# Layer 1 of a two-layer diffusion backbone: projection, latent heads and both attentions as one stage of head pairs

## The chip, the cores and the metric

The kernel runs on one core of a Trainium2 chip. The metric is the device time of one execution in microseconds (us), less being better. The engines are PE (TensorE: matrix products into PSUM; PEld is its load of the stationary operand), DVE (VectorE), ACT (ScalarE), POOL (GpSimd) and SP (SyncE, which here only issues transfers). ACTq, SPq and POOLq are the instruction queues of those engines where they issue a transfer. PSUM has eight banks of 128 partitions by 512 float32 numbers. Everything is float32.

## What is computed

384 tokens (128 context tokens, 256 latent ones on a grid of 4 rows by 64 columns) go through two layers. Each layer is a mixer and then a mixture of 32 experts. The change lies in the mixer of layer 1, which has two attentions of eight heads side by side:

```python
def odd_mixer(h, j, P, cache):
    zq, zkv, zpe, nq, nk, nv = split_cols(h @ P['odd_w_in'][j], ODD_SPLITS)   # 256, 128, 32, 512, 512, 512
    ckv = rmsnorm(zkv, P['mla_kv_a_g'][j])
    q = mla_queries(zq, ...)      # rmsnorm, @ w_q_up (256 x 768), rmsnorm per head of 96, rotation
    k, v = mla_keys(ckv, zpe, ...)  # @ w_kv_up (128 x 1024), rmsnorm per head of 96, rotation
    nq = rmsnorm(nq.reshape(B, T, NAT_HEADS, HEAD_DIM), P['nat_q_g'][j])
    nk = rmsnorm(nk.reshape(B, T, NAT_HEADS, HEAD_DIM), P['nat_k_g'][j])
    y_mla = dense_attention(q, concat([k_c, k]), concat([v_c, v]))
    y_nat = neighbourhood_attention(nq, nk, nv, nk_c, nv_c, P['nat_rpb'][j])
    return concat([y_mla, y_nat]) @ P['odd_w_out'][j]
```

Context tokens attend to the 128 context keys alone, latent tokens to 128 cached keys and the 256 latent ones. In the neighbourhood attention every latent score gets a bias `rpb[head, row distance, column distance]`, and keys outside a window of 16 columns are masked out. The tokens are three tiles of 128 rows (t = 0 context, t = 1, 2 latent), so a unit of attention is one head of one tile: a product of scores (128 queries by 128 or 384 keys), a softmax, and a product with the values.

## The kernel before

All stages of a layer are blocks with one instruction stream per engine; `end_stage` ends one, and the engines meet there. Weights come in units of up to 2 MB through a ring of six slots (`T.ring`), which SP fills in the order of `weight_units`; a slot is filled again when PE has finished the unit in it, so behind the four units of `odd_w_in` and the two of `odd_w_out` come the first units of layer 1's experts. Layer 1's mixer has these stages:

- `stage_projection` (L640 to L750): the square sums of x, three normalized tiles, their transposes (`Turns`, L363, copied out with the modulation at L318 and L322), and then 12 jobs of eight products: unit n of `odd_w_in` by tile t (L739). `OddNorms` normalizes the latents and the neighbourhood queries and keys after the unit that holds them; the power of -0.5 is POOL's (L613).
- `stage_mla_heads` (L1823 to L1966): three groups of transposes of the latents, 6 jobs for the queries (L1957) and 8 for keys and values (L1960), then on DVE the sums, the scaling, the gain and the rotation of q and of k (L1929, L1935, L1938, L993, L997), with POOL for the powers (L1907) and for the cosine products (L1898). Then the transposes of q and k, 16 groups, whose copies ACT and DVE take in turn (L387).
- `stage_mla_attention`: class `Attention` (L827 to L972) for 24 units, one head of one tile each, in software pipeline: scores of unit i (L860), transposes of the probabilities of unit i-1 (L868), values of unit i-2 (L879, the transposed probabilities being the stationary operand). DVE takes the maximum (L936) and the shift (L947), ACT the exponential with its sum (L913), ACT and DVE copy the transposes in turn (L896). After eight heads DVE divides (L972) and writes rows of `mix`. The scores alternate between two banks, so the scores of unit i wait for the exponential of unit i-2.
- `stage_neighbourhood` (L1998 to L2110): transposes of nq and nk, among them of the cached keys, which ACT loads when the stage begins (L2036); 32 small transfers that spread the bias table over the partitions (L2052, 20 on SP, 12 on POOL); then the same `Attention`. In its first eight units `between` puts a product with a flip matrix (L2105) and a DVE pass (L2081) for the bias of two heads of one tile; the first of them waits for all 32 transfers. The scores get the bias in DVE's masked pass (L941).
- `stage_output` (L755): six groups of transposes of `mix`, then the output product (L816) and the gated residual.

Layer 0's window attention already runs on another class, `PairAttention` (L1005 to L1136), which takes two heads at a time with two score banks for both, divides in a diagonal matrix that stands in for the identity in the transpose (L1046, L1114), and writes the result transposed, so that no transposes follow. Products of the projection are put into its gaps.

The first waits of the two kinds of attention are these lines:

```python
if i >= 2:                                             # Attention, two score banks, one per unit
    pe.wait_ge(self.s_prob.sem, self.s_prob.at(i - 1))
...
if i >= 1:                                             # PairAttention, two score banks, both per step
    if self.steps[i - 1][3] is None:
        pe.wait_ge(self.s_prob.sem, self.s_prob.at(i))
```

## Time and profile before

| What | us |
|---|---|
| Median of 2 timed runs | 1868.99 (1868.97 to 1869.01) |
| The profiled execution, its own time | 1868.74 |
| Span of its trace | 1866.9 |
| PE busy in the span | 1416.1 (76%) |
| DVE, ACT, POOL busy | 534.8, 283.4, 246.1 |
| Mean granted PE clock, share of full speed | 0.891 |

Times in the trace are counted from the start of the span; 1.8 us of the execution lie outside it. PE's two clock levels are 1.2 and 2.4 GHz; the granted clock of a stretch is given as a share of the higher one, so 0.50 is the lower. Busy time of PE is that of instructions in flight, and a float32 product is issued as two instructions. The share of an engine is a mean over stages that have different limits, so what a change in one stage is worth has to be read inside that stage.

### The profile page before, as it was taken

The page shows a single profiled execution, that of the slowest core. Times are in us where ns is not written, and L with a number is a line of the kernel's source. Part 1 is how long each engine was busy: PE and PEld are TensorE (multiplying, and loading weights), DVE is VectorE, ACT ScalarE, POOL GpSimd, SP SyncE. Part 2 cuts the span into 40 slices and gives each one's busy share as a digit, 9 for nine tenths or more (in the row PEclk, how much of TensorE's full clock was granted, in tenths as well). Part 3 has the DMA queues.
Part 4 walks back from the last instruction along what each step waited for, and adds up shares of the span by engine and source line. Part 5 has one row for each costly group of instructions (what it writes and reads, how often), then busy time and mean ns, then how long its engine had stood idle before and what let it go on. Part 6 is the DMA issues. An engine that isn't in the chain of part 4 may idle for free. (4 is left out here: it accounts for less than half of the span.)

```text
span 1866.9 us, 19168 instructions
## 1 busy us (share of the span) xinstructions
PE 1416.1 (76%) x7912; PEld 778.7 (42%) x7912; DVE 534.8 (29%) x1013; ACT 283.4 (15%) x664; POOL 246.1 (13%) x237
## 2 busy tenths in 40 slices
PE   4999896749877777778079575998398777777772
PEld 3544443335444444444034253564154444444441
DVE  1142233452222222222222452322522222222222
ACT  2123335101000000000021232211010000000000
POOL 0100000222111111101102302000311111111101
PEclk9999998759999999999579876568599999999996
DMA  9637669329999999999722104002289999999994
GB/s 345 238 114 250 199 215 398 105 83 424 425 426 424 426 425 424 425 422 394 282 75 98 45 2 64 0 35 93 81 343 424 424 425 426 424 424 426 424 410 161
DMA packets 116073, 524.88 MB, mean 281 GB/s; under 512 B 39468, under 2 KB 44524, under 8 KB 91408
## 3 DMA queue, kind: packets, MB, share of 16 engines
q1 hardware_dynamic: 87216, 498.03, 66.1%
q0 software_dynamic: 10752, 13.49, 2.2%
q10 hardware_dynamic: 18016, 12.11, 2.1%
q8 instruction: 64, 1.05, 0.2%
q14 instruction: 25, 0.20, 0.0%
HBM read 521.37 MB, written 23.15 MB: 292 GB/s over the span
## 5 line engine op out<-in xcount | busy, mean ns | idle before, releaser
L2453 PE MATMUL ps<-ring,e_xT 128*64 128x256 f32 x4096 | 493.1, 392 | 120.2 <-DMA ring<-in_moe_w_gate 66.0
L2453 PEld LDWEIGHTS ps<-ring,e_xT 128*64 128x64 f32 x4096 | 303.2, 135 | 332.1 <-issue 118.4
L2467 PE MATMUL ps<-ring,e_hidT 128*64 128x512 f32 x1024 | 235.5, 601 | 53.8 <-DMA ring<-in_moe_w_down 53.8
L2511 POOL DMA_INDIRECT expert_rows<-e_y,table x64 | 64.7, 1011 | 794.9 <-DVE e_y L2628 785.1
L2467 PEld LDWEIGHTS ps<-ring,e_hidT 128*64 128x64 f32 x1024 | 79.4, 137 | 165.6 <-issue 116.5
L2628 DVE COPY e_y<-ps 128x512 f32<-128x512 f32 x64 | 44.3, 692 | 313.8 <-PE ps L2467 313.8
L1334 PE MATMUL ps<-ring,hT 128*128 128x512 f32 (+1 forms) x288 | 119.7, 571 | 5.0 <-ACT hT L318 5.0
L2636 DVE RECIPROCAL e_sig<-e_sig 128x256 f32<-128x256 f32 x64 | 112.2, 1753 | 2.2
L2634 DVE TENSOR_SCALAR e_sig<-e_sig 128x256 f32<-128x256 f32 x64 | 18.9, 295 | 312.9 <-ACT e_sig L2595 312.9
L2595 ACT ACTIVATE e_sig<-ps 128x256 f32<-128x256 f32 x64 | 24.5, 383 | 550.2 <-PE ps L2453 550.2
L739 PE MATMUL ps<-ring,hT 128*128 128x512 f32 (+1 forms) x192 | 81.4, 588 | 1.5 <-ACT hT L318 1.5
L1334 PEld LDWEIGHTS ps<-ring,hT 128*128 128x128 f32 x288 | 54.6, 194 | 61.4 <-issue 54.2
L2505 POOL DMA_INDIRECT x_in<-h_rows,table x64 | 65.8, 1029 | 83.1 <-issue 38.6
L2598 ACT COPY e_hidT<-ps 128x256 f32<-128x256 f32 x64 | 23.8, 372 | 300.3 <-PE ps L2459 300.3
L816 PE MATMUL ps<-ring,mixT 128*128 128x512 f32 x144 | 65.0, 615 | 1.6 <-issue 1.6
L363 PE MATMUL ps<-const,h 128*128 128x128 f32 x48 | 10.5, 401 | 73.3 <-DVE h L718 48.9
L2641 DVE TENSOR_TENSOR e_hid<-e_sig,ps 128x256 f32<-128x256 f32 x64 | 27.0, 421 | 111.0 <-PE ps L2453 111.0
L739 PEld LDWEIGHTS ps<-ring,hT 128*128 128x128 f32 x192 | 37.5, 196 | 45.2 <-issue 43.3
L395 PE MATMUL ps<-ring,cond 128*32 128x512 f32 x384 | 50.6, 648 | 6.9 <-ACT z L424 3.9
L2441 PE MATMUL ps<-const,x_in 128*128 128x128 f32 x256 | 42.8, 291 | 10.2 <-DMA x_in<-h_rows,table 10.2
L816 PEld LDWEIGHTS ps<-ring,mixT 128*128 128x128 f32 x144 | 28.4, 198 | 37.2 <-issue 36.1
L363 PE MATMUL ps<-const,mix 128*128 128x128 f32 (+1 forms) x61 | 14.1, 403 | 39.1 <-DVE mix L997 19.7
(329 smaller groups left out, 1390.4 us busy)
## 6 DMA issues: line engine op xcount, KB each, us to landing
ring<-in_moe_w_gate SPq DMA_DIRECT2D x64, 2048.0 KB, 26.8
ring<-in_moe_w_up SPq DMA_DIRECT2D x64, 2048.0 KB, 26.9
ring<-in_moe_w_down SPq DMA_DIRECT2D x64, 2048.0 KB, 27.0
ring<-in_ada_w SPq DMA_DIRECT2D x24, 2048.0 KB, 11.7
ring<-in_even_w_in SPq DMA_DIRECT2D x5, 2048.0 KB, 18.5
ring<-in_odd_w_in SPq DMA_DIRECT2D x3, 2048.0 KB, 26.6
rows<-expert_rows SPq DMA_DIRECT2D x12, 512.0 KB, 9.1
ring<-in_even_w_out SPq DMA_DIRECT2D x2, 2048.0 KB, 12.0
```

The costliest lines, as they stand in the source:

```text
L395: ins = T.nc.tensor.matmul(T.ps[32 * j:32 * (j + 1), bank, :], T.cond[:, c, :], T.unit(u)[:, c, :], start=(c < 4), stop=(c >= 4))
L739: ins = nc.tensor.matmul(T.ps[:, 4 + e % 4, 0:cols], hT[:, c, t * P:(t + 1) * P], T.unit(first + n)[:, c, :], start=(c == 0), stop=(c == K ...
L816: ins = nc.tensor.matmul(T.ps[:, 4 + e % 4, :], mixT[:, 4 * halves[k] + c, t * P:(t + 1) * P], T.unit(u)[:, c, n * 512:(n + 1) * 512], sta ...
L1334: ins = nc.tensor.matmul(T.ps[:, bank[e], 0:cols], hT[:, c, t * P:(t + 1) * P], T.unit(u)[:, c, :], start=(c == 0), stop=(c == KC - 1))
L2441: ins = nc.tensor.transpose(T.ps[:, 0, c * P:(c + 1) * P], x[:, c::4], T.c("ident"))
L2453: ins = nc.tensor.matmul(T.ps[f * BLK:(f + 1) * BLK, bank, 0:FF // 2].rearrange("p (q b) -> p q b", b=2), mine, weights[:, c, f], start=(c ...
L2467: ins = nc.tensor.matmul(T.ps[n * BLK:(n + 1) * BLK, bank, :], mine, weights[:, j, n * HALF:(n + 1) * HALF], start=(j == 0), stop=(j == FC ...
L2505: nc.gpsimd.indirect_dma_start(out=x_in[:, b % 2, :], out_offset=None, in_=T.h_dram, in_offset=plan.tokens(b), bounds_check=2 * TOK - 1, o ...
L2511: nc.gpsimd.indirect_dma_start(out=T.y_dram, out_offset=plan.targets(done), in_=y[:, done % 2, :], in_offset=None, bounds_check=4 * TOK - ...
L2628: v.tensor_copy(y[:, e % 2, :], T.ps[:, Y_BANK + e % 2, :]).then_inc(y_out.sem, y_out.adds(1))
L2636: v.reciprocal(g, g).then_inc(silu.sem, silu.adds(1))
L2641: v.tensor_tensor(hid[:, s, :], g, up_ps(s), ALU.mult).then_inc(hidden.sem, hidden.adds(1))
```

## The change

`stage_projection`, `stage_mla_heads`, `stage_mla_attention`, `stage_neighbourhood` and the classes `OddNorms`, `MlaTables` and `Attention` go; one `stage_odd` takes their place. Its parts:

- The order of PE's jobs is: units 0 and 1 of `odd_w_in`, the latents' transposes, the query and the key/value products, and only then units 2 and 3.
- All six normalizations are done by a small class: the square on ACT, the sum on DVE, the power of -0.5 as a logarithm and an exponential on ACT (`root`), scaling and gain on DVE, in the order qa, kv, q, nq, k, nk.
- The 24 groups of transposes of q, k, nq and nk stand together behind the jobs. The cached neighbourhood keys and values are loaded early, into columns of z that are free by then. The four stores of new caches are issued among the transposes.
- Both attentions are one run of `PairAttention` over 24 steps of two heads. The scores of a step go to banks 0 and 1, and the scores of the next step wait for this step's exponentials.
- The bias table is loaded by 16 transfers (8 on SP, 8 on POOL, behind the last transposes) of 64 by 6 by 64 numbers instead of 32 of 64 by 4 by 64; both latent tiles take their part from the same copy. The mask is added to it in four DVE passes at steps 4 to 7. The flip matrix, scaled, is applied by PE straight into the score banks, as a second product of each long neighbourhood step.
- The output stage gets its input transposed and has no transposes of its own.

The core of the diff, the output stage's groups, the attention's scores, the list of jobs, the steps and the bias:

```diff
         groups = [([mix[:, t, (4 * k + c) * P:(4 * k + c + 1) * P] for c in range(4)],
-                   mixT[:, 4 * k:4 * k + 4, t * P:(t + 1) * P], None) for t in range(NT) for k in halves]
+                   mixT[:, 4 * k:4 * k + 4, t * P:(t + 1) * P], None) for t in range(NT) for k in halves if mix is not None]
...
-                        pe.wait_ge(self.s_prob.sem, self.s_prob.at(i))
+                step, before = self.steps[i], i - len(self.scores)
+                if before >= 0:
+                    if self.steps[before].mask is None:
+                        pe.wait_ge(self.s_prob.sem, self.s_prob.at(before + 1))
                     else:
-                        pe.wait_ge(self.s_shift.sem, self.s_shift.at(i))
+                        pe.wait_ge(self.s_shift.sem, self.s_shift.at(before + 1))
                 for a in range(2):
-                    ins = nc.tensor.matmul(T.ps[:, a, 0:self.keys(i)], q[a], k[a], start=True, stop=True)
+                    ins = nc.tensor.matmul(self.score_ps(i, a), step.q[a], step.k[a], start=True, stop=(step.added is None))
+                if step.added is not None:
+                    pe.wait_ge(self.added_ready[0].sem, self.added_ready[0].at(self.added_ready[1]))
+                    for a in range(2):
+                        ins = nc.tensor.matmul(self.score_ps(i, a)[:, P:], self.flip, step.added[a], start=False, stop=True)
                 ins.then_inc(self.s_score.sem, self.s_score.adds(1))
...
+        N_LATENT = 3
+        LOADS = 11 * 16
+
+
+        jobs = [("in", n, t) for n in range(2) for t in range(NT)]
+        jobs += [("q", t, half) for t in range(NT) for half in range(2)] + [("kv", t, half) for t in range(4) for half in range(2)]
+        jobs += [("in", n, t) for n in range(2, 4) for t in range(NT)]
+        FIRST_Q, FIRST_KV, LATE_IN = 6, 12, 20
+        copier = [e % 2 if e < LATE_IN else 0 for e in range(len(jobs))]
+        last_of_unit = [job[0] == "in" and job[2] == NT - 1 for job in jobs]
+
...
+        for t in range(NT):
+            for j in range(4):
+                pair = (2 * j, 2 * j + 1)
+                halves = [slice(a * HD, (a + 1) * HD) for a in range(2)]
+                key = key_order(nat_kT[:, j, :])[min(t, 1)]
+                own = [[z[:, s, NV0 + a * HD:NV0 + (a + 1) * HD] for a in pair] for s in range(NT)]
+                before = [[vc[a] for a in pair]]
+                added = None if t == 0 else [bias_area[:, a, (4 - 2 * t) * GRID_W:(8 - 2 * t) * GRID_W] for a in pair]
+                steps_att.append(Step([nat_qT[r, j, t * P:(t + 1) * P] for r in halves], [key[r] for r in halves],
+                                      own[0:1] if t == 0 else before + own[1:], mixT[:, 4 + j, t * P:(t + 1) * P], HD ** -0.5,
+                                      added=added))
+        prob = z[:, 0:2, NQ0:NQ0 + 768].rearrange("p s (a k) -> p s a k", a=2)
+        probT = [z[:, 2, NQ0 + a * 384:NQ0 + (a + 1) * 384] for a in range(2)]
+        diag = z[:, 0, NQ0 + 768:NK0 + 512].rearrange("p (a k) -> p a k", a=2)
+        att = PairAttention(T, steps_att, None, prob, probT, diag, small, scores=((0, 1),), turned=(2, 3), out=6,
+                            flip=flip_near[:, 0:P], added_ready=(biased, HEADS // 2))
...
+        def bias_load(queue, head, half):
+            first = (head * 15 + 5 - half) * RPB_COLS + 15 - (GRID_W - 1)
+            src = bass.AP(tensor=I["nat_rpb"].tensor, offset=I["nat_rpb"].offset + first,
+                          ap=[[1, GRID_W], [RPB_COLS, BLOCKS], [1, GRID_W]])
+            part = slice(half * GRID_W, (half + 1) * GRID_W)
+            return queue.dma_start(bias_area[part, head, :].rearrange("p (k c) -> p k c", k=BLOCKS), src)
+
+        @block.sync
+        def _(sp):
+            T.load_ahead(sp, units[0], units[-1] + 1)
+            sp.wait_ge(turns.done.sem, turns.done.at(len(groups)))
+            for head in range(SP_HEADS):
+                for half in range(2):
+                    bias_load(sp, head, half).then_inc(rows_in.sem, rows_in.adds(16))
+            sp.wait_ge(rows_in.sem, rows_in.now())
 
...
+            dve.wait_ge(stored.sem, stored.at(64))
+
+            def between(i):
+
+                n = i - 4
+                if 0 <= n < HEADS // 2:
+                    if n == 0:
+                        dve.wait_ge(rows_in.sem, rows_in.at(16 * SP_HEADS * 2))
+                        dve.wait_ge(pool_rows_in.sem, pool_rows_in.at(16 * (HEADS - SP_HEADS) * 2))
+                    mask = flip_near[:, P:].unsqueeze(1).broadcast_to([P, 2 * BLOCKS, GRID_W])
+                    two = bias_area[:, 2 * n:2 * n + 2, :].rearrange("p h (k c) -> p (h k) c", c=GRID_W)
+                    vec.tensor_tensor(two, two, mask, ALU.add).then_inc(biased.sem, biased.adds(1))
+
+            att.vector(dve, between)
 
```


**PE, projection and heads of layer 1.** Before (`mla_kT` lends its room to the latents and their weights, `mix` to the queries):

```order
L739 MATMUL ps<-ring,hT 128x512 x72
L739 MATMUL ps<-ring,hT 128x416 x24
L648 UNCONDITIONAL_BRANCH
L1946 UNCONDITIONAL_BRANCH
L363 MATMUL ps<-const,z 128x128 x7
L363 MATMUL ps<-const,mix 128x128
L363 MATMUL ps<-const,z 128x128 x2
L1957 MATMUL ps<-mla_kT 128x384 x12
L1960 MATMUL ps<-mla_kT 128x512 x8
L363 MATMUL ps<-const,mix 96x128 x24
```


Now (`odd_v`, `odd_k_area`, `mixT` and `odd_bias` lend the rooms):

```order
L1867 MATMUL ps<-ring,odd_hT 128x512 x48
L366 MATMUL ps<-const,z 128x128 x7
L366 MATMUL ps<-const,mixT 128x128
L366 MATMUL ps<-const,z 128x128 x2
L1871 MATMUL ps<-odd_k_area 128x384 x12
L1874 MATMUL ps<-odd_k_area 128x512 x8
L1867 MATMUL ps<-ring,odd_hT 128x512 x24
L1867 MATMUL ps<-ring,odd_hT 128x416 x24
L366 MATMUL ps<-const,mixT 96x128 x24
L366 MATMUL ps<-const,odd_bias 96x128 x32
```


Half of the 96 products with `ring` have moved behind the products of the latents, and between those and the transposes of 96 rows.

**DVE, from the last key copies to the first transposes' copies.** Before (L1929 sums, L1935 scales, L1938 gain, L993 and L997 rotation):

```order
L1935 TENSOR_TENSOR mix<-mix,mla_stat_q 128x3x768
L1938 TENSOR_TENSOR mix<-mix 128x3x768
L993 TENSOR_TENSOR mla_qT<-mix,const 128x16x8 x4
L997 TENSOR_TENSOR mix<-z,mla_qT 128x2x8x32
L1935 TENSOR_TENSOR mla_k<-mla_k,mla_stat_k 128x3072
L1938 TENSOR_TENSOR mla_k<-mla_k,mix 128x3072
L993 TENSOR_TENSOR mla_kT<-mla_k,const 128x16x8 x4
L997 TENSOR_TENSOR mla_k<-mla_kT 128x16x32
L387 COPY mla_qT<-ps 96x384 x4
```


Now (L1795 sums, L1801 scales, L1804 gain; L390 copies transposes):

```order
L652 TENSOR_TENSOR odd_nat_area<-mixT,const 128x16x8 x4
L656 TENSOR_TENSOR mixT<-odd_nat_area 128x16x32
L1801 TENSOR_TENSOR odd_bias<-odd_bias,cond 128x3072
L1804 TENSOR_TENSOR odd_bias<-odd_bias,mixT 128x3072
L652 TENSOR_TENSOR odd_nat_area<-odd_bias,const 128x16x8 x4
L656 TENSOR_TENSOR odd_bias<-odd_nat_area 128x16x32
L1801 TENSOR_TENSOR z<-z,odd_small 128x3x512
L1804 TENSOR_TENSOR z<-z,cond 128x3x512
L1795 TENSOR_REDUCE odd_small<-odd_k_area 128x24
L1801 TENSOR_TENSOR z<-z,odd_small 128x3x512
L1804 TENSOR_TENSOR z<-z,cond 128x3x512
L390 COPY odd_hT<-ps 96x384 x4
```


The rotated q and k no longer go straight to the transposes; the neighbourhood queries and keys stand between.

**PE, long steps of the neighbourhood attention.** Before, two heads of a tile (L860 scores, L868 transposes, L879 values):

```order
L860 MATMUL ps<-nat_kT,nat_qT 128x384
L868 MATMUL ps<-const,nat_prob 128x128 x3
L879 MATMUL ps<-nat_vc,nat_probT 128x64
L879 MATMUL ps<-z,nat_probT 128x64 x2
L860 MATMUL ps<-nat_kT,nat_qT 128x384
L868 MATMUL ps<-const,nat_prob 128x128 x3
L879 MATMUL ps<-nat_vc,nat_probT 128x64
L879 MATMUL ps<-z,nat_probT 128x64 x2
```


Now, two steps of two heads each, the values being those of two steps earlier (L714 scores, L718 flip times bias, L729 transposes by the diagonal, L742 values):

```order
L714 MATMUL ps<-odd_nat_area,mixT 128x384 x2
L718 MATMUL ps<-odd_bias,odd_flip_near 128x256 x2
L729 MATMUL ps<-z 128x128 x6
L742 MATMUL ps<-z 64x128 x2
L714 MATMUL ps<-odd_nat_area,mixT 128x384 x2
L718 MATMUL ps<-odd_bias,odd_flip_near 128x256 x2
L729 MATMUL ps<-z 128x128 x6
L742 MATMUL ps<-z 64x128 x6
```


The bias has become a product of each step, and the values' product has 64 stationary and 128 moving columns instead of 128 and 64.

## Rows read from the trace of the kernel before

**Rows 1.** windows of layer 1; columns named in the first line

```profile
core 0: us, PE busy (x) PEld busy (x) DVE busy (x) ACT busy (x) POOL busy (x), PEclk, DMA share, GB/s
951.00:1033.00 82.00, 81.28 (x192) 37.29 (x192) 18.76 (x18) 7.66 (x10) 10.84 (x8) 0.97 0.21 77
1033.00:1051.00 18.00, 16.69 (x50) 8.66 (x50) 6.71 (x11) 7.00 (x14) 1.75 (x6) 1.00 0.32 118
1051.00:1080.00 29.00, 1.51 (x6) 1.05 (x6) 20.14 (x19) 3.24 (x2) 17.11 (x7) 0.57 0.00 0
1093.00:1104.00 11.00, 10.15 (x39) 8.30 (x40) 4.14 (x19) 4.36 (x20) 0.00 (x0) 0.50 0.01 2
1106.00:1134.00 28.00, 27.32 (x174) 20.60 (x172) 16.10 (x43) 13.02 (x38) 0.00 (x0) 0.99 0.00 1
1194.00:1243.00 49.00, 49.00 (x157) 33.49 (x156) 14.60 (x52) 12.45 (x35) 0.00 (x0) 0.50 0.03 9
```

**Rows 2.** longest waits of PE in layer 1 (total, times, longest)

```profile
PE ps L363 <- DVE mix L997: 19.7, 1, 19.7
PE ps L2105 <- DMA nat_bias<-in_nat_rpb: 12.2, 1, 12.2
PE ps L363 <- DMA nat_vc<-in_cache_nat_v: 6.1, 1, 6.1
```

**Rows 3.** timeline, SP's weight loads and PE's first output product (start, us, what)

```profile
994.96 0.35 SPq L270 DMA_DIRECT2D ring<-in_moe_w_up  x1
1032.32 0.33 SPq L270 DMA_DIRECT2D ring<-in_moe_w_up  x1
1252.26 4.10 PE L816 MATMUL ps<-ring,mixT 128*128 128x512 f32 x9 [0.83 <-issue]
```

**Rows 4.** DVE's share of the head stage, one 1536-wide pass, a table load

```profile
1048.00:1080.00 32.00, 4.42 (x13) 2.00 (x11) 23.14 (x22) 4.53 (x6) 17.45 (x8) 0.61 0.00 0
L604 DVE TENSOR_TENSOR z<-z,nat_gains 128x1536 f32<-128x1536 f32 x2 | 3.5, 1758 | 0.1
L1626 ACT ACT_TABLE_LOAD x4 | 5.1, 1283 | 0.3
```

**Rows 5.** transposes alone: a window, one copy at each clock

```profile
1086.00:1092.00 6.00, 3.75 (x29) 2.74 (x27) 2.74 (x4) 2.33 (x4) 0.00 (x0) 1.00 0.04 11
1087.54 0.69 DVE L387 COPY mla_kT<-ps 96x512 f32<-96x512 f32 x1 [0.74 <-PE ps L363]
1148.62 0.69 DVE L387 COPY nat_kT<-ps 128x512 f32<-128x512 f32 x1 [1.21 <-PE ps L363]
```

**Rows 6.** timeline of PE and DVE, a 384-column product and one score

```profile
1039.77 4.03 PE L1957 MATMUL ps<-mla_kT 128*128 128x384 f32 x12
1110.17 0.86 PE L860 MATMUL ps<-mla_kT,mla_qT 96*128 96x384 f32 x2
1111.08 0.56 DVE L936 TENSOR_REDUCE mla_top<-ps 128x1 f32<-128x384 f32 x1 [0.90 <-PE ps L860]
```

**Rows 7.** timeline and a window of layer 0's attention by pairs

```profile
197.74 1.50 PE L1046 MATMUL ps<-room,win_paired 128*128 128x128 f32 x12
202.60 0.32 PE L1059 MATMUL ps<-h,win_vc 128*64 128x128 f32 x1
203.41 0.92 PE L1035 MATMUL ps<-win_kT,h 64*128 64x384 f32 x4
206.45 0.60 ACT L1079 ACTIVATE win_paired<-win_paired,h 128x384 f32<-128x384 f32 x1
212.00:222.00 10.00, 6.16 (x63) 5.07 (x63) 3.28 (x11) 3.46 (x14) 0.61 (x3) 1.00 0.96 354
```

**Rows 8.** timeline, the bias loads of both queues and who waits

```profile
1135.06 22.28 SPq L2052 DMA_DIRECT2D nat_bias<-in_nat_rpb  x20
1135.58 7.55 POOL L2052 DMA_DIRECT2D nat_bias<-in_nat_rpb  x12 [56.73 <-POOLq L1969]
1162.47 2.07 PE L2105 MATMUL ps<-nat_bias,nat_flip_near 128*128 128x512 f32 x2 [12.25 <-DMA nat_bias<-in_nat_rpb]
```

More of the change, by code:

```diff
@@ new lines, in stage_odd @@
+        QA, KV, Q, K, NQ, NK = range(6)
+        ORDER = (QA, KV, Q, NQ, K, NK)
+        squares, rstd, row = T.counter("squares"), T.counter("rstd"), T.counter("rows")
+        product, out = T.counter("product"), (T.counter("z_act"), T.counter("z_dve"))
+        loads, steps, act_steps = T.counter("loads"), T.counter("dve_done"), T.counter("act_done")
+        head_squares, sums, head_rstd = (T.counter("odd_" + n) for n in ("squares", "sums", "rstd"))
+        cached = T.counter("cached_in")
@@ L1909, in _ @@
+            turns.copy_out(act, copy, 0, N_LATENT + 2 * HEADS)
+            act.wait_ge(stored.sem, stored.at(64))
+            att.scalar(act, lambda n: None)
         @block.gpsimd
         def _(pool):
+            g = nc.gpsimd
+            for t in range(NT):
+                one = slice(t, t + 1)
+                pool.wait_ge(squares.sem, squares.at(t + 1))
+                g.tensor_scalar(stat[:, 0, one], stat[:, 0, one], 1.0 / D, EPS, ALU.mult, ALU.add).then_inc(rstd.sem, rstd.adds(1))
+                pool.wait_ge(rstd.sem, rstd.now())
+                g.tensor_tensor(stat[:, 1, one], stat[:, 0, one], T.c("half")[:, 0:1], ALU.pow).then_inc(rstd.sem, rstd.adds(1))
@@ L1920, in _ @@
+            pool.wait_ge(turns.done.sem, turns.done.at(len(groups)))
+            for head in range(SP_HEADS, HEADS):
+                for half in range(2):
+                    bias_load(pool, head, half).then_inc(pool_rows_in.sem, pool_rows_in.adds(16))
+            pool.wait_ge(pool_rows_in.sem, pool_rows_in.now())
         @block.vector
         def _(dve):
-            turns.copy_out(dve, nc.vector.tensor_copy, 1, 0, 3)
-            products_out(dve, nc.vector.tensor_copy, 1, 0, 10)
-            parts = ((q_heads, NT, stat_q, q_room), (k_heads, 4, stat_k, k_room))
@@ L2109, in stage_neighbourhood @@
+            for e in range(len(jobs) - 4, len(jobs)):
+                wait_copied(pe, e)
+            att.tensor(pe, lambda n: None)
     T.end_stage()
```

916 lines of the change are left out of this document (329 added, 587 removed).

## The prediction

> **What bounds the kernel now.** I read the windows of layer 1's mixer first, then PE's waits, then the timeline. The mixer is a serial stretch between the experts of layer 0 and those of layer 1. In its windows the DMA share lies between 0.00 and 0.32 [rows 1], so the weights are no limit there, and what the stretch loses or gains should pass to the whole time. Three things stand out. In 1051 to 1080 PE works 1.5 of 29 us while DVE works 20: PE waits 19.7 us for DVE's rotation of q [rows 1, 2]. Before the neighbourhood attention it waits 6.1 us for the cached keys and 12.2 us for the bias table [rows 2]. And all long units of that attention, 1194 to 1243, run at PE clock 0.50 with PE busy throughout, where the long latent units of 1106 to 1134 run at 0.99 [rows 1]. A long head issues 11 PE records (2 scores, 3 transposes, 6 values), so 28 us x 11 / 174 = 1.8 us per head there, against 49 x 11 / 157 = 3.4 us here.
>
> **The sum, part by part.** I time the changed stretch from the end of weight unit 1, 994.96 [rows 3], to the first output product, 1252.26 [rows 3]: 257.3 us before. What lies ahead of 994.96 keeps its work; one more load is issued on ACT there, about 0.35 us by the issue in rows 3, and I take 0.5.
>
> 1. Latents, query and key products: 18.0 us [rows 1], unchanged. The three latent groups now wait for a root on ACT with two table loads of 1.28 us per norm [rows 4], but those run while PE works on the rest of unit 1; I take nothing for it (0 to 3).
> 2. Units 2 and 3: 1032.32 - 994.96 = 37.4 us [rows 3], the same work in a later place. PE is done at 994.96 + 0.5 + 18.0 + 37.4 = 1050.9. Nothing is saved so far; the gain is what DVE does meanwhile.
> 3. DVE's chain starts at 1013.5. In 1048 to 1080 DVE was busy 23.1 us, some 2.1 of it five copies of 0.4 us, so q and k cost 21.0 us [rows 4]. nq and nk, with a sum, a scaling and a gain of 1536 columns each, add 6 x 1.76 = 10.5 us [rows 4]. Waits in the chain (squares, table loads, POOL's cosines): the same window has 32.0 - 23.1 = 8.9 us of idle time, and I take 9 (3 to 15). The chain ends at 1013.5 + 31.5 + 9 = 1054, so of PE's long wait about 3 us are left. Cover: 37.4 us of products. Were it gone, the whole 40.5 us would lie open.
> 4. 24 groups of transposes. One copy of DVE and the idle time before it are 0.69 + 0.74 = 1.43 us per two groups at full clock [rows 5]: 12 x 1.43 = 17.2 us. ACT issues four stores among its copies, 4 x 0.33 [rows 3] = 1.3 us. End: 1054 + 18.5 = 1072.5. Stores land under the remaining groups, and the cached keys come under the products; their 6.1 us go.
> 5. A long step of two heads is a chain, since the next scores need this step's exponentials. One score with its way to DVE is 1111.08 - 1110.17 = 0.91 us [rows 6]; the second head's adds 4.03 / 12 x 2 = 0.67 [rows 6]; the maximum over twice 384 columns about 1.0 (0.56 for one [rows 6]); shift and hops 0.25; two exponentials 1.2 (0.60 each [rows 7]): 4.05 us. PE's own work in a latent step is 1.34 for scores, 1.50 for the diagonal transposes, 203.41 - 202.60 = 0.8 for values [rows 7], together 3.65, so it hides behind the chain. In a neighbourhood step the two scores use different halves of the rows: four records are through in 0.92 us [rows 7]. The bias adds two products of 256 columns, 2 x 0.45 = 0.9. Chain: 0.91 + 0.9 + 1.0 + 0.25 + 1.2 = 4.25 us. At the lower clock PE's work doubles to 7.3 and 7.7 us and is the bound.
> 6. Short steps: 8 short heads and the first long score fill the 11.0 us of 1093 to 1104 at the lower clock [rows 1]; 2.6 us per step there, 2.2 at full clock (an estimate; 1.5 to 2.6).
> 7. The clock. It fell before while PE waited, and stayed low through the short latent units and 2 us more (0.50 to 1104, 0.99 from 1106 [rows 1]). I let the short latent steps run low, and add 3 us once for each attention, one long step at half speed. Layer 0's pairs kept 1.00 in 212 to 222 with PE busy only 6.2 of 10 us [rows 7]; that is the nearest row for whether long pair steps keep it.
> 8. The bias table. 20 loads of 64 x 4 pieces were issued in 22.28 us on SP, and PE got them 27.4 us after the first [rows 8], so 5.1 us behind the last issue. Now 8 loads of 64 x 6 pieces: 8 x 1.11 = 8.9 us if the cost is per load, 13.4 if per piece; ready 14 to 18.5 us after the last transpose. DVE asks for them in step 4 of the latent attention, after 4 x 2.6 + 2.7 = 13 us. Behind that wait stand, on DVE, the copy of the transposes of step 3 and everything after it; PE and ACT wait for both. I take 4 us (0 to 14). The four mask passes of 768 columns, about 0.9 us each by half of the 1.76 [rows 4], lie in DVE's slack of the long latent steps, 4.05 - 2.4 = 1.6 us.
> 9. Attention: 4 x 2.6 + 4 + 3 + 8 x 4.05 + 4 x 2.2 + 3 + 8 x 4.25 + 6 for draining the pipeline (one diagonal, transposes, copies, two products of values, an estimate of 4 to 8) = 101.6 us, to 1174.1.
> 10. Output: no transposes; 1 us for the change of stage (0.83 us of idle time stands in rows 3 for a start of this kind). First product at 1175.1 instead of 1252.3: 77 us saved.
>
> The sum is made against the profiled execution: 1868.74 - 77.2 = 1791.5. That execution is 0.25 us under the median of the runs shown, so 1792 in their terms.
>
> **A rule against row 4.** In 1086 to 1092 PE did nothing but transposes, and the granted clock was 1.00 [rows 5]. The Trainium skill ("TensorE: Matmul & The Clock Gate", Part 4: PE-mode transpose) says that transposes do not count as PE being busy in the way that products do and that full speed does not engage for them. By that rule the 24 groups would run low. Two groups then take 0.69 + 1.21 = 1.90 us as in 1148 [rows 5], 12 x 0.47 = 5.6 us more, and the sum would be 1797; the row speaks against it, and I leave the term as it is.
>
> **Rivals.**
>
> - Low clock in the neighbourhood attention. For it: before, PE was busy without a gap there and stayed at 0.50 for 49 us [rows 1]; four short steps come first. Against it: the heads now fill all rows together, the bias products and diagonal transposes are full ones, and the pairs of layer 0 kept 1.00. Price: 8 x (7.7 - 4.25) - 3 = 25 us: 1817.
> - Low clock in both attentions, entered by the wait for the table. Another 8 x (7.3 - 4.05) - 3 = 23: 1840.
> - The table takes as long as before, 27.4 us [rows 8], since pieces and not loads decide and two queues share the engines: the wait in step 4 is 27.4 - 13 = 14 us instead of 4: 1802.
> - Slower than before: the single set of score banks serializes everything. Scores, maximum, exponentials, diagonal, transposes, copies and values of one step would follow one another with no overlap, at the lower clock, because PE runs its queue in order and stands at the transposes that wait for the diagonal. A long step would be 2.7 + 0.25 + 1.0 + 0.2 + 1.2 + 0.65 + 3.0 + 0.6 + 1.6 + 0.3 = 11.5 us, a short one about 5; 16 x 11.5 + 8 x 5 + 6 = 230, the first output product at 1303: 51 us later than before, 1920. It decides from (1252.3 - 1 - 1072.5 - 40 - 6) / 16 = 8.3 us per long step on. Against it: the queue order has the scores of the next step ahead of these transposes, and the diagonal needs only 0.65 us of DVE time while the scores run.
> - The hiding of item 3 fails: a job of unit 2 or 3 is held by its copy on ACT, which has squares and roots ahead of it, or the chain is 20 us longer. PE waits about 20 us more: 1812. Against it: a job needs only the bank of four jobs earlier.
>
> **Chances.** The forecast (full clock in most long steps) 0.62, low clock in one attention 0.15, in both 0.06, table late 0.08, hiding fails 0.06, slower 0.03. The range is 1778 to 1832: the lower end takes no wait for the table, 1.5 us short steps, the shorter waits in item 3 and draining, and the upper end holds all cases but the low clock in both attentions and the slower one. A measurement of this kernel tells some 2% from no change, 37 us; faster than that means under 1831.6. From the cases: faster 0.91, within 2% 0.06, slower 0.03.
>
> **What would show it.** Right: the window behind the last key product has PE busy for 37 us; PE waits under 6 us for DVE before the transposes; DVE's first score of a long latent step comes every 4 us and of a long neighbourhood step every 4.3; granted clock near 1.00 there; one wait of DVE for the table of some microseconds; no product with the flip matrix outside the score banks. Wrong: a period of 7 us or more with clock 0.50 (first two rivals); DVE idle over 10 us in step 4; PE's transposes in line behind each step's copies (serial rival); a saving in the trace of the mixer that the expert stage of layer 1 takes back by waiting for its weights, which would make the forecast wrong though each step is right.

## The result, and the profile after

| | before | changed |
|---|---|---|
| Median of 2 timed runs, us | 1868.99 | 1783.75 (1783.14 to 1784.36) |
| Ratio | | 0.9544 (95% interval 0.9503 to 0.9585) |
| Profiled execution, its span, us | 1868.74, 1866.9 | 1784.36, 1782.5 |
| Mean granted PE clock | 0.891 | 0.922 |

The forecast was 1792 (1778 to 1832), faster with 0.91; the changed kernel is 85.2 us faster. In five further executions it was 1783.17 (1781.6 to 1784.3), with a ratio of 0.9543 (0.9530 to 0.9556). One thing is needed to read the numbers below: of 36 executions of the kernel before that ran beside the experiments, 31 took 1865 to 1873 us, one 1861 and four 1832 to 1837, and beside those four I compare medians and traces instead of ratios.

The stretch that the prediction times, from the end of weight unit 1 to the first output product, has these ends in the changed kernel (timeline, start, us, what):

```profile
994.67 0.35 SPq L273 DMA_DIRECT2D ring<-in_moe_w_up  x1
1032.85 0.33 SPq L273 DMA_DIRECT2D ring<-in_moe_w_gate  x1
1049.61 0.33 SPq L273 DMA_DIRECT2D ring<-in_moe_w_up  x1
1067.98 1.99 SPq L1674 DMA_DIRECT2D odd_bias<-in_nat_rpb  x3
...
1167.97 7.53 PE L624 MATMUL ps<-ring,mixT 128*128 128x512 f32 x17 [0.75 <-PEq L1512]
```

1167.97 - 994.67 = 173.3 us against 257.3 in [rows 3]: 84.0 saved, where 77.2 were forecast. What follows is unchanged: from the first output product to the end of the span it is 614.5 us now and was 614.6. The loads at 1032.85 and 1049.61 are released by the ends of units 2 and 3, so PE's products end at 1049.6, and the load at 1067.98, the first of the bias table, by the last transpose.

The windows of the changed kernel, beside [rows 1]:

```profile
core 0: us, PE busy (x) PEld busy (x) DVE busy (x) ACT busy (x) POOL busy (x), PEclk, DMA share, GB/s
1033.00:1050.00 17.00, 17.00 (x54) 9.43 (x52) 14.95 (x11) 6.31 (x9) 1.57 (x2) 1.00 0.34 123
1050.00:1060.00 10.00, 6.46 (x38) 4.57 (x36) 5.60 (x8) 2.92 (x7) 0.00 (x0) 0.83 0.59 210
1060.00:1064.00 4.00, 2.90 (x23) 2.16 (x23) 1.93 (x3) 1.42 (x3) 0.00 (x0) 1.00 0.18 67
1064.00:1068.00 4.00, 3.51 (x22) 2.28 (x22) 1.86 (x3) 1.56 (x4) 0.00 (x0) 1.00 0.28 89
1068.00:1080.00 12.00, 9.19 (x38) 7.03 (x39) 5.48 (x20) 4.82 (x22) 5.45 (x8) 0.65 0.76 124
1080.00:1090.00 10.00, 8.90 (x32) 5.78 (x32) 4.96 (x10) 2.98 (x11) 0.00 (x0) 0.57 0.07 10
1090.00:1116.00 26.00, 23.32 (x179) 17.76 (x179) 16.18 (x37) 11.43 (x41) 0.00 (x0) 1.00 0.01 2
1140.00:1160.00 20.00, 18.50 (x141) 13.85 (x138) 9.52 (x23) 7.21 (x25) 0.00 (x0) 1.00 0.00 1
```

The 29 us in which PE worked 1.5 are gone. In the kernel before they were the 19.7 us of [rows 2] and, right behind, a wait of PE for the first copies of the transposes:

```profile
PE ps L363 <- DVE mla_qT L387: 8.3, 1, 8.3
```

In 1033 to 1050 PE is now busy throughout while DVE works 15 of 17 us beside it. The clock is low in three places: for some 3 us of the transposes (0.83 in 1050 to 1060), in 1068 to 1090, the short latent steps and the first two long ones, and for some 3 us near 1130, in the second long neighbourhood step. It is 1.00 in the later long neighbourhood steps (1140 to 1160), where [rows 1] had 0.50 over 49 us. PE's longest waits, which answer to [rows 2], are now (total, times, longest):

```profile
PE ps L714 <- ACT z L761: 10.0, 18, 1.7
PE ps L729 <- DVE z L796: 3.2, 4, 1.3
PE ps L366 <- DVE odd_hT L390: 3.1, 3, 2.4
```

The first is the price of the single set of score banks: 18 times the scores stand for the exponentials of the step before. The third is what is left of DVE's chain.

### The profile page after: what moved, and what is told of

It is laid out like the page before. It is cut to its first block and busy times, and to the rows that moved or that the text cites. A ratio compares the mean times of both kernels' runs of the same rounds, so it can differ in the third digit from the quotient of the medians.

```text
span 1782.5 us, 19309 instructions
## 1 busy us (share of the span) xinstructions
PE 1368.3 (77%) x8016; PEld 753.1 (42%) x8016; DVE 532.1 (30%) x975; ACT 303.1 (17%) x712; POOL 216.9 (12%) x219
## 5 line engine op out<-in xcount | busy, mean ns | idle before, releaser
L1017 PE MATMUL ps<-ring,hT 128*128 128x512 f32 (+1 forms) x288 | 121.1, 576 | 4.9 <-ACT hT L321 4.9
L1867 PE MATMUL ps<-ring,odd_hT 128*128 128x512 f32 (+1 forms) x192 | 81.3, 586 | 1.5 <-ACT odd_hT L321 1.5
L1017 PEld LDWEIGHTS ps<-ring,hT 128*128 128x128 f32 x288 | 54.9, 195 | 62.5 <-issue 55.3
L1867 PEld LDWEIGHTS ps<-ring,odd_hT 128*128 128x128 f32 x192 | 37.4, 195 | 45.0 <-issue 43.1
L366 PE MATMUL ps<-const,odd_v 128*128 128x128 f32 x24 | 5.9, 423 | 56.5 <-DVE odd_v L1810 49.2
L2228 PEld LDWEIGHTS ps<-const,x_in 128*128 128x128 f32 x256 | 36.7, 210 | 11.4 <-DMA x_in<-h_rows,table 10.6
```

Source lines behind the costliest of these rows:

```text
L1017: ins = nc.tensor.matmul(T.ps[:, bank[e], 0:cols], hT[:, c, t * P:(t + 1) * P], T.unit(u)[:, c, :], start=(c == 0), stop=(c == KC - 1))
L1867: ins = nc.tensor.matmul(bank(e)[:, 0:cols], hT[:, c, b * P:(b + 1) * P], T.unit(u)[:, c, :], start=(c == 0), stop=(c == KC - 1))
L2228: ins = nc.tensor.transpose(T.ps[:, 0, c * P:(c + 1) * P], x[:, c::4], T.c("ident"))
```

## The experiments

Each kernel was timed in four executions (the last in five), one of them profiled. Stretch means the time from the end of unit 1 to the first output product in the profiled execution, 257.3 before and 173.3 in the changed kernel.

**The order of the jobs undone** (e1_order):

```diff
-        jobs = [("in", n, t) for n in range(2) for t in range(NT)]
+        jobs = [("in", n, t) for n in range(4) for t in range(NT)]
...
-        jobs += [("in", n, t) for n in range(2, 4) for t in range(NT)]
-        FIRST_Q, FIRST_KV, LATE_IN = 6, 12, 20
+        FIRST_Q, FIRST_KV, LATE_IN = 6, 12, 26
```

> The changed kernel with units 2 and 3 ahead of the query and key products again; every job's copy alternates between ACT and DVE. Theory A (the units cover DVE's chain): PE has done its products at 1050 as before, DVE's chain, 1012.6 to 1052.1 now, starts at 1050 and ends near 1089, PE waits 35 to 39 us in one piece for q and k, and the time is 1783.75 + 36 = 1820 (1813 to 1828; the upper part if the clock stays at 0.50 through the transposes behind the wait). Theory B (the gain comes from the pairs and the clock, the chain would have been short anyway): PE waits under 12 us, under 1796.

Measured 1822.53 us (1821.6 to 1823.2), ratio to the kernel before 0.9743 (0.9727 to 0.9760); stretch 211.15. PE's waits in it:

```profile
PE ps L366 <- issue: 19.7, 1, 19.7
PE ps L366 <- DVE odd_hT L390: 18.9, 1, 18.9
```

Together 38.6 us in which PE has nothing but two groups of transposes between them. Theory A holds: the cover is worth 1822.5 - 1783.75 = 38.8 us, 37.9 in the stretch, about the 37.4 us of products that provide it. PE's waits grew by 36.2 (38.6 against 2.4); the clock behind them is low (0.66 in 1090 to 1100), which may be the rest. Theory B falls.

**Roots on POOL** (e9_roots_on_pool):

```diff
-            root(QA)
-            root(KV)
...
+            def power(n):
+                s = norms[n].stat
+                pool.wait_ge(sums.sem, sums.at(ORDER.index(n) + 1))
+                g.tensor_scalar(s[:, 0, :], s[:, 0, :], 1.0 / norms[n].width, EPS, ALU.mult, ALU.add).then_inc(act_steps.sem, act_steps.adds(1))
+                pool.wait_ge(act_steps.sem, act_steps.now())
+                g.tensor_tensor(s[:, 1, :], s[:, 0, :], T.c("half")[:, 0:s.shape[2]], ALU.pow).then_inc(head_rstd.sem, head_rstd.adds(1))
```

> The changed kernel with the power of -0.5 of all six norms on POOL, as before the change, instead of a logarithm and an exponential with two table loads on ACT. Theory A (roots on ACT, 3.1 us each with their table loads, are what keeps DVE's chain within the cover of units 2 and 3): by the POOL rows of the kernel before (4.2 us for 24 columns, 7.7 for 32) the keys' power ends near 1037 where DVE asks for it at 1032, the cosine products queue behind it, and the last power takes 1.3 us more than the root; the chain ends 7 to 10 us later, PE's waits for DVE ahead of the transposes grow from 2.4 to about 10 us, 1792 (1789 to 1794). Theory B (the roots lie beside other work on either engine): under 1786.

Measured 1792.51 us (1792.4 to 1794.1), 8.8 us over the changed kernel. In its timeline DVE waits for the cosine products, which stand on POOL behind the power of the keys, and for the last power:

```profile
1038.47 0.69 DVE L656 TENSOR_TENSOR mixT<-odd_nat_area 128x512 f32<-128x512 f32 x1 [6.10 <-POOL odd_nat_area L1787]
1058.24 1.76 DVE L1810 TENSOR_TENSOR z<-z,odd_small 128x1536 f32<-128x1536 f32 x1 [4.58 <-POOL odd_small L1768]
```

and PE's longest wait in it before the transposes is

```profile
PE ps L366 <- DVE odd_hT L390: 9.8, 1, 9.8
```

Theory A holds. The chain has no slack left: counted from the end of unit 1, the last scaling starts 7.1 us later than in the changed kernel (61.0 against 53.9 us), and PE's longest wait grew by 7.4 us.

**Two sets of score banks** (e2_two_sets):

```diff
-        att = PairAttention(T, steps_att, None, prob, probT, diag, small, scores=((0, 1),), turned=(2, 3), out=6,
+        att = PairAttention(T, steps_att, None, prob, probT, diag, small, scores=((0, 1), (4, 5)), turned=(2, 3), out=6,
```

> The changed kernel with two sets of score banks, (0, 1) and (4, 5), taken in turn. Theory A (a long step is a chain through the single set): the scores of the next step no longer wait for the exponentials, a long step takes PE's own work, 1.34 + 1.50 + 0.9 = 3.7 us instead of 4.08 in the latent attention and 0.85 + 1.0 + 1.45 + 0.9 = 4.2 instead of 4.50 in the neighbourhood one, a short step some 0.4 us less: 8 x 0.4 + 8 x 0.3 + 7 x 0.3 = 7.7 us, 1776 (1771 to 1780). Theory B (the order of DVE's work sets the period: it takes the next maximum only behind the diagonal of this step): periods within 0.1 us of 4.08 and 4.50, 1783.75 +- 2.

Measured 1775.15 us (1773.7 to 1777.3), ratio to the kernel before 0.9489 (0.9473 to 0.9505); stretch 164.96, 8.3 us shorter. The maxima of two consecutive steps, of the latent and of the neighbourhood attention, in this kernel:

```profile
1104.53 0.96 DVE L803 TENSOR_REDUCE odd_small<-ps 128x2 f32<-128x768 f32 x1 [0.32 <-PE ps L714]
1108.22 0.96 DVE L803 TENSOR_REDUCE odd_small<-ps 128x2 f32<-128x768 f32 x1 [0.32 <-PE ps L714]
...
1145.91 0.96 DVE L803 TENSOR_REDUCE odd_small<-ps 128x2 f32<-128x768 f32 x1 [0.74 <-PE ps L718]
1149.96 0.96 DVE L803 TENSOR_REDUCE odd_small<-ps 128x2 f32<-128x768 f32 x1 [0.74 <-PE ps L718]
```

and in the changed kernel:

```profile
1103.59 0.96 DVE L803 TENSOR_REDUCE odd_small<-ps 128x2 f32<-128x768 f32 x1 [0.77 <-PE ps L714]
1107.67 0.96 DVE L803 TENSOR_REDUCE odd_small<-ps 128x2 f32<-128x768 f32 x1 [0.76 <-PE ps L714]
...
1146.17 0.96 DVE L803 TENSOR_REDUCE odd_small<-ps 128x2 f32<-128x768 f32 x1 [1.19 <-PE ps L718]
1150.66 0.96 DVE L803 TENSOR_REDUCE odd_small<-ps 128x2 f32<-128x768 f32 x1 [1.19 <-PE ps L718]
```

Periods 3.69 and 4.05 instead of 4.08 and 4.49: PE's own work instead of the chain, for PE is now busy 20.0 of the 20 us from 1130 to 1150. Theory A holds, and B falls.

**Without the bias products** (e3_no_bias_product; the scores get neither bias nor mask, loads and mask passes stay):

```diff
-                                      added=added))
+                                      added=None))
```

> The changed kernel without the bias products (the scores get no bias and no mask; loads and mask passes stay). Theory A (they cost their own time and no more): a long neighbourhood step takes 3.5 to 3.7 us instead of 4.50, granted clock 1.00 as now, 8 x 0.9 = 7 us less, 1777 (1774 to 1779). Theory B (scores on half the rows let the clock fall, and these products on all 128 rows are what holds it): granted clock 0.50 over the long neighbourhood steps, about 6.4 us per step, 15 us more, 1799 (1790 to 1805).

Measured 1777.37 us (1775.5 to 1779.1), 6.4 us less; stretch 164.22, 9.1 us shorter. The later long neighbourhood steps follow each other at 3.69 us, 0.8 less than with the products. The clock falls once, to 0.50 in 1128 to 1131, as in the changed kernel's trace, and is back at 0.98 in the next 3 us. A window of this kernel, and two maxima of its timeline:

```profile
1140.00:1160.00 20.00, 15.39 (x146) 11.81 (x144) 9.35 (x22) 8.44 (x27) 0.00 (x0) 1.00 0.00 1
```

```profile
1144.03 0.95 DVE L803 TENSOR_REDUCE odd_small<-ps 128x2 f32<-128x768 f32 x1
...
1147.72 0.95 DVE L803 TENSOR_REDUCE odd_small<-ps 128x2 f32<-128x768 f32 x1
```

Theory A holds. The bias products are not what keeps the clock up in pair steps. The products with the diagonal still fill all 128 rows here, and two scores use the two halves of the rows, so this run does not show what part of the form does.

**The bias table in 32 loads** (e4_32_loads; each load split in two halves of three pieces):

```diff
+            n = BLOCKS // 2
-                          ap=[[1, GRID_W], [RPB_COLS, BLOCKS], [1, GRID_W]])
+                          ap=[[1, GRID_W], [RPB_COLS, n], [1, GRID_W]])
```

> The changed kernel with the bias table in 32 loads of 64 x 3 pieces instead of 16 of 64 x 6, the same pieces in all. Theory A (a load costs its issue, whatever its pieces): SP issues 16 x 1.15 = 18.4 us instead of 9.2, the last piece lands near 1090, DVE waits for it from 1082.9 for 5 to 9 us in step 4, the clock is low there: 1791 (1787 to 1796). Theory B (the pieces cost, not the loads): SP's issues stay near 9.2 us in all, DVE waits under 1 us, 1783.75 +- 2.

Measured 1784.99 us (1782.3 to 1786.6): neither a gain nor a loss that can be told. Issues on both queues and DVE's wait, in this kernel:

```profile
1069.14 12.90 SPq L1676 DMA_DIRECT2D odd_bias<-in_nat_rpb  x16
1069.42 9.90 POOL L1676 DMA_DIRECT2D odd_bias<-in_nat_rpb  x16 [27.79 <-PE ps L366]
1085.85 0.96 DVE L1855 TENSOR_TENSOR odd_bias<-odd_bias,odd_flip_near 128x768 f32<-128x768 f32 x1 [1.17 <-DMA odd_bias<-in_nat_rpb]
```

On SP neither theory holds: 16 loads of half the size took 12.9 us (0.81 each), 8 whole ones 9.2 (1.15 each), so a load has a part of its own and a part that goes with its pieces. On POOL 0.62 against 0.68 each: there nearly all goes with the load. The wait of 1.2 us shows how near the table is: the changed kernel's DVE asked for it 14.9 us after the first issue and found it there.

**The kernel before without its bias loads** (b1_no_tables; POOL fills the table with zeros, so the output has no bias):

```diff
-                    bias_load(sp, h, r).then_inc(tables.sem, tables.adds(16))
...
-            nc.gpsimd.memset(bias[:, :, :, 0:P], 0.0).then_inc(zeroed.sem, zeroed.adds(1))
+            nc.gpsimd.memset(bias[:, :, :, :], 0.0).then_inc(zeroed.sem, zeroed.adds(1))
```

> The kernel before without its 32 bias loads: POOL fills the table with zeros at the start of the neighbourhood stage, so PE's wait of 12.2 us goes (the bias is zero, the mask stays). Everything else of that attention is as it was. Theory C (its clock of 0.50 over 1175 to 1243 is left over from the waits ahead of it): the granted clock of the long units is 1.00, they take 28 instead of 49 us, and with the wait 1869 - 12 - 21 = 1836 (1825 to 1845). Theory F (the form of the units, single heads with scores on 64 rows, holds it low): clock 0.50 there as before, 1869 - 12 = 1857 (1852 to 1860).

**The kernel before with scores on all 128 rows** (b2_full_rows; the scores are sums of two heads):

```diff
-                k = key_order(kT[rows, h // 2, :])[min(t, 1)]
+                k = key_order(kT[:, h // 2, :])[min(t, 1)]
...
-                units.append((qT[rows, h // 2, t * P:(t + 1) * P], k, values, mask, HD ** -0.5))
+                units.append((qT[:, h // 2, t * P:(t + 1) * P], k, values, mask, HD ** -0.5))
```

> The kernel before with neighbourhood scores over all 128 rows (the scores are sums of two heads; the number of instructions and of columns is the same). The waits stay. Theory C (clock left over from the waits): 0.50 over the long units as before, 1869 +- 2. Theory F (scores on 64 rows hold it low): granted clock near 1.00 over the long units, 28 instead of 49 us, 1848 (1843 to 1855).

The first took 1815.1, 1814.9, 1816.0 and once 1853.05 us; the second 1829.6 to 1830.8 in all four. The kernel before beside them took 1868.2 to 1870.7, and once 1836.25. Windows without the loads, then with full rows:

```profile
1145.00:1175.00 30.00, 29.47 (x138) 16.95 (x138) 17.85 (x59) 11.40 (x40) 0.00 (x0) 1.00 0.00 1
1175.00:1190.00 15.00, 14.51 (x86) 10.04 (x86) 7.92 (x28) 7.12 (x20) 0.00 (x0) 1.00 0.03 9
```

```profile
1162.00:1168.00 6.00, 5.70 (x13) 3.54 (x14) 2.25 (x7) 0.74 (x4) 0.00 (x0) 0.50 0.00 0
1168.00:1175.00 7.00, 6.95 (x30) 4.14 (x29) 4.64 (x15) 2.33 (x12) 0.00 (x0) 0.98 0.00 0
1175.00:1194.00 19.00, 18.19 (x110) 12.85 (x108) 11.97 (x43) 8.95 (x28) 0.00 (x0) 1.00 0.01 2
```

Neither theory alone is right, and both times lie below the ranges given (1825 to 1845 and 1843 to 1855), for the first eight units of that attention, which ran at 0.50 too in the kernel before (1162 to 1194), gained as well. The same single heads on 64 rows run at 1.00 when they are entered without the wait (C), and after the full wait of 11.6 us at 0.50 the clock comes back by 1168 when the scores fill all rows (F). So that attention could keep either clock, and the wait ahead of it mostly put it on the lower one. The outcomes lie 33 us (1869 against 1836) and 38 us (1853 against 1815.5) apart. No trace of an execution of 1836 or of 1853 us was taken, so that these have the same cause is inferred from the size.

**Order of the steps and of DVE's copies.** Three kernels with two sets of banks and one with the single set. Late scaling of the neighbourhood keys (e5_late_nk), long latent steps first (e6_long_first, and e8_long_first_one_set with the single set), each short step between two long ones (e7_mixed):

```diff
             total(NK)
+            turns.copy_out(dve, copy, 1, N_LATENT, N_LATENT + HEADS)
             scale(NK, nat_ready)
-            turns.copy_out(dve, copy, 1, N_LATENT)
+            turns.copy_out(dve, copy, 1, N_LATENT + HEADS)
```

```diff
+        m, n = steps_att[:12], steps_att[12:]
+        steps_att = m[4:] + m[:4] + n
```

```diff
+        steps_att = [s for a in range(4) for s in (m[4 + 2 * a], m[a], m[5 + 2 * a])]
+        steps_att += [s for a in range(4) for s in (n[4 + 2 * a], n[a], n[5 + 2 * a])]
```

> Two sets of score banks, and DVE copies its half of the query groups before it scales the neighbourhood keys (3.5 us), not behind that. Theory A (PE's wait of 2.4 us for DVE at the start of the transposes is the end of DVE's chain): the first copies come some 2.5 us earlier and DVE, busy half of the time in the transposes, catches up with the 3.5 us; 2 us less than with two sets alone, 1773 (1771.5 to 1774.5). Theory B (the 3.5 us come back at the ninth group): 1775 +- 1.

1776.93 us (1775.4 to 1777.8) against 1775.15: nothing gained. The first copy came 2.1 us earlier after the last product (0.3 us behind it instead of 2.4), but PE then waited at the ninth group for the keys' copy, as theory B says. PE's longest wait in this kernel's transposes:

```profile
PE ps L366 <- DVE odd_k_area L390: 3.2, 2, 2.9
```

> Two sets of score banks, and the four short latent steps moved behind the eight long ones, so that all eight short steps stand together in the middle. Theory A (the clock falls because PE stands idle for much of a short step, and the two long steps behind pay for it): the long latent steps follow the transposes at granted clock 1.00 with 3.7 us each, 2.6 us less for the four short steps and 1.3 us less for the first long ones, 4 us less than with two sets alone, 1771 (1769 to 1773), if the eight short steps together do not lower it ahead of the neighbourhood attention; if they do, 2 to 3 us of it come back there, 1774. Theory B (the clock falls at the change from transposes to attention, whatever the first steps are): the long steps run low for a time, 3.3 us more in each, 1778 or more.

1771.34 us (1771.0 to 1773.7), stretch 159.15: the fastest kernel of the study, 12.4 us under the changed one. No window that I read from the transposes to 1150 is below 1.00; these are two of them:

```profile
1070.00:1075.00 5.00, 2.63 (x12) 1.51 (x11) 2.67 (x5) 1.23 (x4) 4.31 (x7) 1.00 0.57 97
1075.00:1080.00 5.00, 4.92 (x39) 3.77 (x38) 2.72 (x8) 2.94 (x10) 0.00 (x0) 1.00 1.12 179
```

> Two sets of score banks, and each short step put between two long ones (long, short, long, four times in each attention). Theory A (idle time of PE in short steps in a row is what lowers the clock): granted clock 0.95 to 1.00 throughout, a short step costs about 2.0 us between long ones instead of 2.3 to 2.8, 5 to 6 us less than with two sets alone, 1770 (1767 to 1773). Theory B as for the kernel with the long steps first: low clock behind the transposes, 1776 or more.

1780.81 us (1779.6 to 1781.3): worse than two sets alone, and both theories miss part of it. One short step behind one long was enough for the clock to fall (0.72 in 1070 to 1075, 0.59 in 1075 to 1080), and later, at 1.00, a period of long, short, long took 10.35 us, that is 3.0 for the short step, for PE stands for the diagonal of the long step, which DVE makes only when the exponentials of both its heads are through, and the short step's scores (0.7 us) do not fill that time. Its timeline in such a place:

```profile
1104.81 0.71 PE L714 MATMUL ps<-odd_k_area,odd_hT 96*128 96x128 f32 x4
1106.19 1.58 PE L729 MATMUL ps<-z 128*128 128x128 f32 x12 [0.67 <-DVE z L796]
```

> The changed kernel, one set of score banks, with the four short latent steps moved behind the eight long ones. Theory A (the low clock at the start of the attention comes from the short steps there and costs the first steps): granted clock 1.00 behind the transposes, the short steps 2.1 to 2.5 us each instead of 2.3, 2.8, 2.8 and 4.5 with the first long one, the first long step 4.1 instead of 5.4 us: 4 us less than the changed kernel, 1779.5 (1777.5 to 1781). Theory B (the short steps cost the same wherever they stand, and low clock follows them): 1783.75 +- 1.5, with the clock low after the eight short steps.

1781.96 us (1778.2 to 1785.0 in four executions): inconclusive as a time. The profiled execution, the slowest of the four, shows 0.79 and 0.53 in 1070 to 1080 although long steps stand there, and 0.66 in 1120 to 1130 behind the eight short ones. So the order alone does not keep the clock in every execution; in the one trace with two sets, where PE has no wait between long steps, it did (e6). One trace of each cannot show that the second set is the reason.

> The changed kernel as it is, in more executions. The kernel before took 1832 to 1837 us in 4 of the 27 executions beside these experiments, 1861 in one and 1865 to 1872 in the others. Theory A (that split comes from its neighbourhood attention, which runs its scores on 64 rows with single heads and keeps either clock; the pairs come back to full clock each time): all executions of the changed kernel lie within 1779 to 1788. Theory B (the changed kernel has such a split too): one or more executions 10 us or more from the others.

Median 1783.17 us, 1781.6 to 1784.3 in five executions: theory A. The nine executions of the kernel before beside it took 1864.7 to 1872.9.

## Why the prediction was right, step by step

The mechanism and the place of each gain were as forecast. The 7 us more are the sum of errors of both signs: the end of DVE's chain came 2 us earlier than forecast, the transposes took 2.6 less and what follows them 2.6 less. By the prediction's own items:

- Items 1 and 2, right: products end at 1049.6, 1050.9 forecast. The three latent groups' roots on ACT cost nothing to be seen.
- Item 3, its end right within 2 us by two errors that partly cancel: DVE's first copy of a group starts at 1052.05, 1054 forecast. The waits behind the first sum are 1.23, 0.28 and 1.92 us, with 2.19 ahead of it 5.6 and not 9; the work from 1013.0 to that copy is then 39.0 - 5.6 = 33.4 us and not 31.5. PE waits 2.4 us in one piece (3 forecast). Undoing the cover cost 38.8 us (e1), where the item gives 40.5 - 3 = 37.5.
- Item 4, 2.6 us too large: the 24 groups end at 1068.0, 15.9 us behind 1052.05, and 18.5 was forecast. The period at full clock is the one of [rows 5]:

```profile
1059.15 0.69 DVE L390 COPY odd_k_area<-ps 96x512 f32<-96x512 f32 x1 [0.74 <-PE ps L366]
1060.57 0.69 DVE L390 COPY odd_k_area<-ps 96x512 f32<-96x512 f32 x1 [0.73 <-PE ps L366]
```

  but only twelve of the 24 groups have 512 columns; two groups of 384 took 1.18 us (6 x 1.43 + 6 x 1.18 = 15.7), and the item took 1.43 for all. The 1.3 us for the four stores did not show in the time. The clock was at 0.50 for some 3 us in between and rose again while PE did nothing but transposes:

```profile
1056.00:1057.00 1.00, 0.90 (x5) 0.49 (x4) 0.48 (x1) 0.44 (x1) 0.00 (x0) 0.50 0.31 131
1058.00:1059.00 1.00, 0.86 (x8) 0.47 (x6) 0.41 (x1) 0.58 (x1) 0.00 (x0) 1.00 0.00 0
```

  The rule of the Trainium skill ("TensorE: Matmul & The Clock Gate", Part 4: PE-mode transpose) that full speed does not engage for transposes is contradicted a second time by this rise and by 1060 to 1068, which holds transposes alone, at 1.00 and 1.00.
- Item 5, its size right for the latent steps (4.08 measured, 4.05 forecast). A long neighbourhood step took 4.49, 4.25 forecast: from the first record of the scores to the maximum it is 1144.15 to 1146.17, 2.0 us, where the item had 1.81. That is 8 x 0.24 = 2 us too little.
- Items 6 and 7: four short latent steps fill 1068.7 to 1078.9, 2.55 us each, as forecast. The penalty behind them was as forecast too: from 1078.87, the first long scores, to the first neighbourhood scores is 35.4 us, 2.7 more than 8 x 4.08, where 3 were forecast. The four short neighbourhood steps were sized too small: they fill 10.6 us, 2.64 each at clock 1.00, where the item had 2.2:

```profile
1114.23 0.49 PE L714 MATMUL ps<-odd_nat_area,mixT 64*128 64x128 f32 x4 [0.37 <-ACT z L761]
1124.80 0.92 PE L714 MATMUL ps<-odd_nat_area,mixT 64*128 64x384 f32 x4 [0.28 <-ACT z L761]
```

  The first two of them carry the transposes and values of the last long steps (3.2 and 2.8 us from scores to scores), and only the last takes 2.1. In the neighbourhood attention the clock's penalty is one period of 5.87 instead of 4.49, 1.4 and not 3. Its eight long steps come to 37.3 us against 37.0 forecast, which is luck: the bias term too small and the clock term too large. In the trace of e10 that penalty is absent (all periods 4.50).
- Item 8, the wrong one: 4 us of waiting forecast, none found. DVE takes the first mask pass right behind the shift:

```profile
1082.83 0.17 DVE L813 TENSOR_SCALAR odd_small<-odd_small 128x2 f32<-128x2 f32 x1
1082.91 0.96 DVE L1851 TENSOR_TENSOR odd_bias<-odd_bias,odd_flip_near 128x768 f32<-128x768 f32 x1
```

  The cost per load was right (1.15 us on SP, 9.2 for the 8), but both ends of the sum were off. The pass comes 14.9 us after the first issue and not 13, for the item left out 0.7 us ahead of the first scores and the maximum and the shift of step 4, 1.1 us. And the transfers were through some 13.5 us after the first issue, ahead of the 14 to 18.5 forecast (DMA share and GB/s in the last two columns):

```profile
1081.00:1081.50 0.50, 0.50 (x2) 0.29 (x1) 0.00 (x0) 0.00 (x0) 0.00 (x0) 0.50 0.14 32
1081.50:1082.00 0.50, 0.50 (x3) 0.41 (x2) 0.16 (x1) 0.00 (x0) 0.00 (x0) 0.50 0.00 0
```

  With twice the loads the wait appeared (1.2 us, e4).
- Items 9 and 10: from 1067.98, the end of the transposes, to 1167.97 it is 100.0 us where the items have 102.6. The table's 4 us are missing, draining took about 1 us less, and the short neighbourhood steps and the 0.7 us ahead of the first scores took some of it back.

The rivals: low clock in one or both attentions did not come. The kernel with a single set of banks does serialize, as the slower rival says, but only the scores behind the exponentials: 10 us in 18 waits, and 8.3 us of time (e2), not 7 us per step. The table was not late, and the hiding held.

Where the 84 us came from is less even than the forecast's sum lets it seem. In stretches: the cover of DVE's chain is 37.9 (211.15 - 173.3). The kernel before without the bias loads, its neighbourhood attention at full clock (b1, timeline), has 1198.47 - 995.41 = 203.06:

```profile
995.41 0.35 SPq L270 DMA_DIRECT2D ring<-in_moe_w_up  x1
...
1198.47 4.10 PE L816 MATMUL ps<-ring,mixT 128*128 128x512 f32 x9 [0.83 <-issue]
```

So the low clock and the waits ahead of that attention were worth 257.3 - 203.06 = 54.2; 16.9 of it is the wait of 12.2 us for the table, gone, and that for the cached values, 1.4 instead of 6.1. If both are taken from 257.3, 165.2 is left, and the changed kernel has 173.3: all the rest of the change, the pairs in place of single heads included, costs some 8 us by this sum, which supposes that the terms add and which no single run shows. That rest contains a gain, the output stage's transposes, which took 5.8 us in b1 (1192.71 to 1198.47), so the pairs alone would cost more. The rows agree in direction: with the clock at 0.99 two heads of the latent attention took 2 x 28 x 11 / 174 = 3.5 us [rows 1], and a pair step takes 4.08. Two sets of banks bring it to 3.69 and give the 8.3 us back. So by this estimate the pair form as changed does not gain by being faster. What is left for it is that it came back to full clock each time it was traced, that its result needs no transposes, and that the table has time to land. How much of the clock's gain goes to the form and how much to the missing wait is open: no run puts the pair steps of the neighbourhood attention behind a long wait, and b1 gets full clock without pairs. And the 85 us hold against what the kernel before mostly took; against its four executions of 1832 to 1837 us the changed kernel is some 50 us faster.

## What to carry to other kernels

Look for the longest stretch in which one engine computes alone, and for products that do not depend on it: moving two weight units behind the products that feed DVE's chain hid 38 us, and since the chain then has no slack, every edit must be measured against its length and not against DVE's busy share. Where a new form of a loop trades a pair of buffers for one shared set, read the waits for the engine that empties it; a second set cost two free banks and gave 8 us. And before a gain in a stage at low clock is credited to the new form, run the old one without the wait ahead of it.

## What the runs showed of the hardware that I had not expected

- The same program can keep either clock in a stage and differ by 33 us: four of 36 executions of the kernel before took 1832 to 1837 us, and one of four without the bias loads 1853 instead of 1815.
- Whether the clock comes back behind a wait went with the form of the work and not with PE's being busy: 49 us of busy records at 0.50 [rows 1], against a return within 6 us of the wait when the scores filled 128 rows (b2). Which part of the form decides is open: pair steps without the bias products also came back to 1.00 (e3), but their two scores fill both halves of the rows together.
- The price of a short step depends on its neighbours: 2.1 us in a row at full clock, 2.8 at the lower one, 3.0 between two long ones (e7).
- Transposes alone ran at 1.00 for 8 us, and the clock rose from 0.50 to 1.00 while PE did nothing else (1057 to 1059).
